# Two decoder blocks on one core: first activations before a weight unit is split, transposes of x inside the last output product, and the last columns in two pieces

## The reference

```python
def swiglu(x, w_gate, w_up, w_down):
    return (jax.nn.silu(x @ w_gate) * (x @ w_up)) @ w_down

x = x + FFN_RES * swiglu(rms_norm_2(x, ffn1_norm[l]), ffn1_w_gate[l], ffn1_w_up[l], ffn1_w_down[l])
u = rms_norm_2(x, mix_norm[l]) @ w_in[l]
...
x = x + jnp.concatenate([a_out, b_out], axis=-1) @ w_out[l]
x = x + FFN_RES * swiglu(rms_norm_2(x, ffn2_norm[l]), ffn2_w_gate[l], ffn2_w_up[l], ffn2_w_down[l])
...
return rms_norm_2(x, final_norm)
```

## Time and profile before

| | us |
|---|---|
| median of 3 runs | 1010.57 (1010.52 to 1012.03) |
| the profiled execution, its own time | 1009.01 |
| span of the profiled execution | 1007.0 |
| TensorE busy in the span | 994.0 (99%) |
| VectorE busy | 573.2 (57%) |
| ScalarE busy | 506.3 (50%) |
| GpSimd busy | 63.0 (6%) |

### The profile page before, as it was taken

How to read it: one execution, slowest core, us unless ns; L and a number is a source line. 1 busy time by engine, 2 the same in 40 slices (tenths; PEclk the granted TensorE clock), 3 DMA queues, 4 the chain that set the end, 5 groups by cost and what they waited for, 6 DMA issues and landing times.

```text
span 1007.0 us, 12918 instructions
## 1 busy us (share of the span) xinstructions
PE 994.0 (99%) x4744; PEld 820.9 (82%) x4744; DVE 573.2 (57%) x772; ACT 506.3 (50%) x704; POOL 63.0 (6%) x93
## 2 busy tenths in 40 slices
PE   9999999999999999999999999999999999999997
PEld 6888888888888888888878888888888878888886
DVE  6545655577765455555775454546556575555544
ACT  7545555644374444435673434345567464444433
POOL 3100100020020000000120000001112000000000
PEclk9999999999999999999999999999999999999999
DMA  9755455434475554544555565645562245656531
GB/s 345 241 172 170 161 168 169 140 126 167 168 259 195 174 202 167 192 183 171 184 167 202 174 203 172 203 133 166 193 204 68 84 158 177 202 175 199 175 125 43
DMA packets 98721, 175.64 MB, mean 174 GB/s; under 512 B 5920, under 2 KB 54128, under 8 KB 98672
## 3 DMA queue, kind: packets, MB, share of 16 engines
q1 hardware_dynamic: 97024, 171.53, 50.4%
q0 software_dynamic: 1344, 3.19, 1.1%
q10 hardware_dynamic: 304, 0.27, 0.1%
HBM read 173.91 MB, written 1.05 MB: 174 GB/s over the span
## 4 chain that ended last, share of the span: by engine, by line
PE 96%; DVE 2%; ACT 1%; issue 1%; POOL 0%; POOLq 0%; ACTq 0%; DVEq 0%
PE bank L505 86%; PE bank L519 5%; PE bank L564 1%; PE bank L563 1%; DVE w_lo L1439 1%; PE bank L575 0%; PE bank L948 0%; ACT w_hi L1024 0%; PE bank L886 0%; PE bank L887 0%; PE bank L885 0%; PE bank L619 0%; PE bank L577 0%; PE bank L576 0%; ACT junk L1054 0%
## 5 line engine op out<-in xcount | busy, mean ns | idle before, releaser
L1439 DVE TENSOR_TENSOR w_lo<-raw,w_hi 128x2048 fp32r<-128x2048 f32 (+1 forms) x162 | 365.7, 2262 | 217.9 <-ACT w_hi L1024 217.8
L1024 ACT ACTIVATE w_hi<-raw 128x2048 fp32r<-128x2048 f32 (+1 forms) x162 | 306.3, 1894 | 152.9 <-PE bank L505 152.0
L505 PE MATMUL bank<-w_hi,hA_hi 128*128 128x512 f32 (+1 forms) x880 | 343.0, 396 | 0.1
L505 PE MATMUL bank<-w_hi,hA_lo 128*128 128x512 f32 (+1 forms) x880 | 336.7, 388 | 0.0
L505 PE MATMUL bank<-w_lo,hA_hi 128*128 128x512 f32 (+1 forms) x880 | 336.2, 388 | 0.0
L505 PEld LDWEIGHTS bank<-w_hi,hA_lo 128*128 128x128 f32 x880 | 165.1, 188 | 34.7
L505 PEld LDWEIGHTS bank<-w_lo,hA_hi 128*128 128x128 f32 x880 | 165.4, 188 | 32.2
L505 PEld LDWEIGHTS bank<-w_hi,hA_hi 128*128 128x128 f32 x880 | 164.6, 188 | 33.2 <-DVE hA_lo L1457 0.9
L505 PE MATMUL bank<-w_hi,fT_hi 128*128 128x512 f32 x296 | 91.4, 390 | 0.0
L505 PE MATMUL bank<-w_lo,fT_hi 128*128 128x512 f32 x296 | 91.2, 389 | 0.0
L505 PE MATMUL bank<-w_hi,fT_lo 128*128 128x512 f32 x296 | 91.2, 389 | 0.0
(11 more groups left out here) (264 smaller groups left out, 785.4 us busy)
## 6 DMA issues: line engine op xcount, KB each, us to landing
raw<-in_w_in SPq DMA_DIRECT2D x74, 512.0 KB, 4.7
raw<-in_w_ff SPq DMA_DIRECT2D x64, 512.0 KB, 3.9
raw<-in_ffn_w_gate SPq DMA_DIRECT2D x44, 512.0 KB, 3.8
raw<-in_ffn_w_up SPq DMA_DIRECT2D x44, 512.0 KB, 4.7
raw<-in_ffn_w_down SPq DMA_DIRECT2D x44, 512.0 KB, 3.9
raw<-in_w_out SPq DMA_DIRECT2D x16, 512.0 KB, 3.9
raw<-in_w_branch_diff SPq DMA_DIRECT2D x8, 512.0 KB, 3.7
raw<-in_w_branch_ret SPq DMA_DIRECT2D x8, 512.0 KB, 3.6
```

The source lines that it names most:

```text
L505: mm = pe.matmul(o, a, w, start=first and t == 0 and m < len(outs), stop=last and t == n - 1 and m >= len(todo) - len(outs))
L1024: act.activation(w_hi[u % HI_SLOTS][:, 0:w], raw[u % RAW_SLOTS][:, 0:w], ACT.Copy).then_inc(hi_ready, 1)
L1439: vec.tensor_tensor(w_lo[u % RAW_SLOTS][:, 0:w], raw[u % RAW_SLOTS][:, 0:w], w_hi[u % HI_SLOTS][:, 0:w].bitcast(f32), ALU.subtract).then_i ...
```

## The change

1. In both gated stages ScalarE's `silu(0, 1)` comes before `hi(u + 4)`, and VectorE's `multiply(0, 1)` before `lo(u + 4)`.
2. TensorE does row t = 0 of `output(3, 1)` before the transposes of `src_turn("ffn2", 0)` and row t = 1 after them.
3. On VectorE the low part of f2's first unit comes before `pair_y("l", 3)`, ahead of the last attention columns; that of its second stays behind `split(("cat", 1))`.
4. On ScalarE `hi(U0["f2"] + 1)` comes before `split(("cat", 1))`, and the squares of "ffn2" come behind the split of their token block.
5. At the end the columns 512 to 1023 of token block 1 are two pieces of 256. The last piece's sum of the last two units is formed in another PSUM bank (6), so VectorE's addition for the second piece covers all of 512 to 1023 (what earlier units summed), and that for the third adds bank 6. The mean of squares is joined from three parts.

```diff
+LAST = ((0, HALF), (HALF, HALF + SUB), (HALF + SUB, D))
...
+    last_sum = lambda c0: bank[6] if c0 > HALF else acc(1, c0 // HALF)
...
-                for c in range(2):
+                for c0, c1 in LAST:
+                    out = last_sum(c0)[:, 0:c1 - c0]
                     for w, k0 in ((v + 2, 2 * ((i - 1) % 2)), (v + 3, 2 * (i % 2))):
                         for t in range(2):
-                            todo = product([acc(1, c)[:, :]], fT, k0 + t, 1, w, t * D + c * HALF)
+                            todo = product([out], fT, k0 + t, 1, w, t * D + c0)
                             for m, (o, a, b) in enumerate(todo):
-                                mm = pe.matmul(o, a, b, start=False, stop=(w, t, m) == (v + 3, 1, 2))
+                                mm = pe.matmul(o, a, b, start=c0 > HALF and (w, t, m) == (v + 2, 0, 0),
+                                               stop=(w, t, m) == (v + 3, 1, 2))
                     mm.then_inc(last_half, 1)
...
         output(3, 0).then_inc(acc_done, 1)
+        output(3, 1, t1=1)
         src_turn("ffn2", 0)
-        output(3, 1).then_inc(unit_used, 1)
+        output(3, 1, t0=1).then_inc(unit_used, 1)
...
             silu(0, 0)
+            silu(0, 1)
             hi(u + 4)
-            silu(0, 1)
...
+        hi(U0["f2"] + 1)
         split(("cat", 1))
-        hi(U0["f2"] + 1)
+        split_rows("ffn2", 0)
         squares("ffn2", 0)
-        split_rows("ffn2", 0)
         hi(U0["f2"] + 2)
+        split_rows("ffn2", 1)
         squares("ffn2", 1)
-        split_rows("ffn2", 1)
...
-        act.wait_ge(half_squared, 1)
-        half_square(1)
-        act.wait_ge(x_gain, 4)
+        for n in (1, 2):
+            act.wait_ge(half_squared, n)
+            last_square(n)
+        act.wait_ge(x_gain, 2 + len(LAST))
...
             multiply(0, 0)
+            multiply(0, 1)
             lo(u + 4)
-            multiply(0, 1)
...
+            for n, (c0, c1) in enumerate(LAST):
+                vec.wait_ge(last_half, n + 1)
+                xs, end = x[:, 1, c0:c1], D if n == 1 else c1
+                vec.scalar_tensor_tensor(out=x[:, 1, c0:end], in0=last_sum(c0)[:, 0:end - c0], scalar=0.5,
+                                         in1=x[:, 1, c0:end], op0=ALU.mult, op1=ALU.add).then_inc(half_added, 1)
...
+                vec.wait_ge(half_added, n + 1)
+                vec.tensor_tensor(xg[:, 1, c0:c1], xs, gain[:, c0:c1], ALU.mult).then_inc(x_gain, 1)
...
             pair("l", j, j == MH // 2 - 1)
+            if j == 3:
+                lo(U0["f2"])
             pair_y("l", j)
...
         split(("cat", 1))
-        lo(U0["f2"])
         lo(U0["f2"] + 1)
```

More of the change, by code:

```diff
@@ L207, in two_blocks @@
     g_col = sb("g_col", [P, 96])
-    ss2 = sb("ss2", [P, 4])
+    ss2 = sb("ss2", [P, 8])
     at[0] = -(-at[0] // LINE) * LINE
@@ L337, in two_blocks @@
     last_half, half_added, half_squared = sem("last_half"), sem("half_added"), sem("half_squared")
-    x_gain, mean_ready, scaled = sem("x_gain"), sem("mean_ready"), sem("scaled")
+    x_gain, mean_part, mean_ready, scaled = (sem(n) for n in ("x_gain", "mean_part", "mean_ready", "scaled"))
     out_done = sem("out_done")
@@ L972, in output @@
             return products([acc(tb, c)[:, :] for c in range(2)], hA, 2 * O2_ROWS[n], t1, tb, U0["o2"] + n, D,
-                            n == 0, n == 3, t0=t0)
+                            n == 0, n == 3 and t1 == 2, t0=t0)
         def output_step(n, tb):
@@ L1404, in _, with last_square @@
         squares("final", 0)
-        def half_square(c):
-            act.wait_ge(half_added, c + 1)
+        def last_square(n):
+            c0, c1 = LAST[n]
+            act.wait_ge(half_added, n + 1)
             act.wait_ge(square_sum, SQ["final", 0] + 1)
-            act.activation(junk[:, c * HALF:(c + 1) * HALF], x[:, 1, c * HALF:(c + 1) * HALF], ACT.Square,
-                           accum_out=ss2[:, c:c + 1]).then_inc(half_squared, 1)
-        half_square(0)
+            act.activation(junk[:, c0:c1], x[:, 1, c0:c1], ACT.Square, accum_out=ss2[:, n:n + 1]).then_inc(half_squared, 1)
+        last_square(0)
         act.wait_ge(x_gain, 2)
         act.activation(src[:, 0, :], xg[:, 0, :], ACT.Copy, scale=inv_rms("final", 0)).then_inc(scaled, 1)
-        act.wait_ge(half_squared, 1)
-        half_square(1)
-        act.wait_ge(x_gain, 4)
+        for n in (1, 2):
+            act.wait_ge(half_squared, n)
+            last_square(n)
+        act.wait_ge(x_gain, 2 + len(LAST))
         act.activation(src[:, 1, CUT:D], xg[:, 1, CUT:D], ACT.Copy, scale=inv_rms("final", 1)).then_inc(scaled, 1)
@@ L1783, in final_norm @@
                 by_gain(0, c)
[L1784 to L1791, removed]
+            for n, (c0, c1) in enumerate(LAST):
[3 more added lines that the diff above has]
+                                         in1=x[:, 1, c0:end], op0=ALU.mult, op1=ALU.add).then_inc(half_added, 1)
+                if n:
+                    vec.wait_ge(half_squared, n)
+                    if n == 2:
+                        vec.wait_ge(mean_part, 1)
+                    part = vec.tensor_scalar(ss2[:, 4:5], ss2[:, 0:1], 1.0 / D, EPS, ALU.mult, ALU.add) if n == 1 else \
+                        vec.scalar_tensor_tensor(out=ss2[:, 5:6], in0=ss2[:, 1:2], scalar=1.0 / D, in1=ss2[:, 4:5],
+                                                 op0=ALU.mult, op1=ALU.add)
+                    part.then_inc(mean_part, 1)
+                vec.wait_ge(half_added, n + 1)
+                vec.tensor_tensor(xg[:, 1, c0:c1], xs, gain[:, c0:c1], ALU.mult).then_inc(x_gain, 1)
             n = SQ["final", 1]
-            vec.wait_ge(x_gain, 4)
-            vec.wait_ge(half_squared, 2)
-            vec.scalar_tensor_tensor(out=ms[:, n:n + 1], in0=ss2[:, 1:2], scalar=1.0 / D, in1=ss2[:, 2:3],
+            vec.wait_ge(half_squared, len(LAST))
+            vec.wait_ge(mean_part, 2)
+            vec.scalar_tensor_tensor(out=ms[:, n:n + 1], in0=ss2[:, 2:3], scalar=1.0 / D, in1=ss2[:, 5:6],
                                      op0=ALU.mult, op1=ALU.add).then_inc(mean_ready, 1)
+            vec.wait_ge(x_gain, 2 + len(LAST))
             vec.wait_ge(rstd_ready, n + 1)
```

## The result

The changed kernel takes **1003.40 us** (median of 6 runs, 1003.08 to 1003.69). The kernel before, run beside it, took 1010.55 (6 runs, 1008.74 to 1012.03). The ratio is 0.9929, with a 95% interval of 0.9919 to 0.9938: 7.15 us less, where 5.22 were forecast. The sign was right. The time lies 0.4 us under the lower end of the range.

The account below looks back on a forecast made before the run. TensorE was taken to bound the kernel, with time to win only at two waits and the end chain. 2.64 + 2.37 + 0.21 = 5.22 us less than the median of 1010.57 gave 1005.35 us, range 1003.8 to 1007.9.

Parts of the forecast that it names:

- What bounds the kernel: Whole kernel: TensorE is 99% busy; only its waits for act_f (2.4 us) and x (2.0 us) and the end chain can yield.
- Edit 1, 2.64 us: Start of f1: the second act_f comes in time, TensorE's wait goes and the next matmul starts 2.64 us earlier.
- Edits 2 to 4, 2.37: Before f2: the addition to x is in time, TensorE's wait goes and f2 begins 2.37 us earlier.
- the even cover of f2's first low block: Start of f2: first low block of x done at 812.4, wanted by TensorE at 812.48; nothing booked, 0.3 us kept for range.
- Edit 5, 0.21: End: narrower last pieces shorten the last addition and squares by more than the matmuls lose, 0.21 us won.
- The pace of 0.120 us: End: matmuls of 256 columns start every 0.120 us, by the line through 288 and 512 columns.
- the last of the sum: Whole kernel: the median stays 1.56 us above the profiled execution, so 1003.8 becomes 1005.35 us.
- the clock rival: f2 stage: without rest TensorE's clock falls; 20 us at the lower level would give 1015.4 us; chance 0.04.
- wait at f1's first down product: Rival at f1: VectorE is late with fT_lo, 2.3 us are given back, 1007.6 us; chance 0.09.
- moved waits: Rival at f1 and f2: waits only move to the next product and the first low block, about 1010 us; chance 0.05.
- matmul of 256 columns at the pace of its load: Rival at the end: narrow matmuls take 0.173 us each, 1.3 us more than counted, 1006.6 us; chance 0.04.
- the second rival: At the end: narrow matmuls run at the pace of their weight loads, 0.173 us each, 1006.6 us; chance 0.04.

Follow-up runs that it names:

- r5: Changed kernel with the low part of f2's first unit put back behind the last attention columns on VectorE: 1004.43 us.
- r6: Changed kernel with ScalarE's old order before f2 (squares of x ahead of the high parts, second unit's high part later): 1003.90 us.
- r3: Kernel before with only the last columns cut into two pieces of 256: 1010.12 us.
- r4: Kernel before with both TensorE waits kept but filled with ten and eight matmuls that nobody reads: 1008.85 us.
- r9: Changed kernel with the last columns cut into 320 and 192 instead of 256 and 256: 1003.42 us.
- r0: Kernel before, unchanged, measured again with a profile: 1010.71 us.
- r1: Kernel before with only the second activation and multiplication moved ahead of the fifth unit in both gated stages: 1007.84 us.
- r2: Kernel before with only the three reorderings before f2 (TensorE's output row, VectorE's low part, ScalarE's order): 1007.59 us.
- r7: Changed kernel with the last columns in two halves of 512 again: 1003.94 us.
- r10: Changed kernel with the old order of second activation and multiplication in f2 alone, kept new in f1: 1003.59 us.

## Why the prediction was right and wrong

**What bounds the kernel** was right as far as it went: two waits of TensorE and the chain at the end. What it lacked is the fall of the clock that mostly follows a wait.

**Edit 1, 2.64 us:** the trace gives 2.63, and the foretold times of `act_f`, `fT_lo` and the down product hold within 0.1 us. **Edits 2 to 4, 2.37:** 2.35. Their inner reasons were tested: without edit 3 the wait shifts (r5). Edit 4 had no term of its own in the sum, but the even cover of f2's first low block hangs on it: without it the kernel is 0.5 us slower (r6). **Edit 5, 0.21:** 0.33 by the trace, (1003.85 - 998.26) - 5.26 from the issue of the last output transfer on SyncE before and after, less the shift that stands at the last stage's 512-wide matmuls (995.21 - 989.95). The addition and the squares were taken 0.10 us too long together, from rows of other operations at f1. The time outside the span fell too, from 2.01 to 1.75 us, as in r3 (1.8), which my sum did not hold. The pace of 0.120 us was exact. The smaller one by the Trainium skill (TensorE: Matmul & The Clock Gate, Back-to-back issue gap), an estimate of 0.109 us, was not seen. That section keeps its formula for isolated matmuls and says that beside weight loads, which every matmul has here, the spacing is set by both, so the prediction should not have held it up against these.

Together the profiled executions differ by 5.86 us: 0.45 by the start and small drifts before f1, 2.55 at and after f1 (0.08 of the 2.63 is given back on the way), 2.35 before f2, less 0.09 within it, 0.33 at the end, and 0.26 outside the span. 1003.8 was the forecast for this execution's own time, and 1003.15 it was.

**The step that failed** is the last of the sum: "The median of the runs is 1.56 us above it, 1010.57, which gives 1005.35". I carried that difference over as if it belonged to the machine. It belonged to the two waits: in the median run one of them is followed by 3.4 us at 1.2 GHz, which cost 1.48 to 1.62 us in three traces. r4 took just that away and got 1008.85. From there to 1003.40 is 5.45 us, near the 5.22 of the sum. The forecast was 1.95 us too high: 1.31 of it is this step (1.56 carried over, 0.25 measured). The other 0.65 stands in the profiled execution (1003.8 against 1003.15), mainly the earlier start and drifts, 0.45, and the time outside the span, 0.26. The start varies between executions, so that part of the miss is chance.

The same error stands in the clock rival: "two waits in 1007 us were no rest either, and every slice is at the top level". That was read from one execution, which was one without a fall, as only 8 of the 65 are. The rival turned the mechanism round, too: the clock was at stake in the kernel before, not after. The clues were there: runs from 1010.5 to 1012.0 beside a profiled 1009.0, and two waits of the length in question. The range reached down only to the profile's own forecast, 1003.8, since I had no case in which the gap closes.

The other rivals did not come: no wait at f1's first down product, no moved waits, and no matmul of 256 columns at the pace of its load. At 192 columns they start later than the line says (r9). Whether their loads hold them there, as the second rival has it, no run shows.

## What to carry to other kernels

A wait of about 2 us on TensorE can cost nearly twice its length: look behind it, in windows of a few us with the granted clock, and in more than one execution. Where the median stands above the profiled run, ask what varies before carrying the difference over, and where a wait can't be removed, try filling half of it with matmuls nobody reads. An edit that only gives another its cover (the low part moved up, the squares moved back) has no price of its own in such a sum, but was worth 0.5 to 1.0 us beside it (r6, r5).

## What the runs showed of the hardware

The low stretches behind a wait were of one length: 3.4 us in r0 (f1), in r1 and in r3 (x), from windows of half a us. They began 0.4 to 1.1 us after TensorE had started again (r1 at 808.8, its transposes at 808.36; r0 at 521.4 and 520.50; r3 at 812.1 and 811.01), with no wait in them.

Matmuls with their own weight load start every 0.2264 us at 512 columns, 0.133 at 288, 0.120 at 256, 0.146 at 320 (r9) and 0.110 at 192. Down to 256 that is a line; at 192 they start 0.017 us later than it says, and the cause is open.

GpSimd's mean and power of one element per partition take 0.19 and 0.56 us in the kernel before. In the changed kernel they fell into two subtractions of VectorE, and took 2.29 and 2.48:

```profile
816.99 4.48 DVE L1445 TENSOR_TENSOR w_lo<-raw,w_hi 128x2048 fp32r<-128x2048 f32 x2
...
817.04 2.29 POOL L1976 TENSOR_SCALAR ms<-ss 128x1 f32<-128x1 f32 x1 [5.06 <-ACT junk L1059]
819.41 2.48 POOL L1977 TENSOR_TENSOR rs<-ms,nhalf 128x1 f32<-128x1 f32 x1
```

The mean lasts as long as the first subtraction, and the power ends at 821.89, behind the second (821.47). Before, VectorE had no subtraction under way at that place. The second activation of f2 waited 1.44 us for them, and TensorE did not. The Trainium skill (SBUF — State Buffer, Terms) says that VectorE and GpSimd share a port pair which one holds for a whole instruction while the other is blocked, and the rows agree.

r6 comes near to a test of it. It is the changed kernel with the squares earlier, so both GpSimd instructions end (815.13) before the subtractions begin (817.70), and they take 0.19 and 0.56 us again:

```profile
814.29 0.19 POOL L1976 TENSOR_SCALAR ms<-ss 128x1 f32<-128x1 f32 x1 [4.76 <-ACT junk L1059]
```

In r2, r5, r7, r9 and r10, which have edit 4, they take 2.29 and 2.48 or 2.49. Not every instruction of VectorE does it: in the changed kernel the same two take 0.18 and 0.57 us at 811.14 for token block 0, beside the addition to x (811.08, 1.28 us), which reads one of its operands from PSUM.
